# Layer 1's neighbourhood attention: query tiles of 8 rows by 16 columns, doubled buffers, and the normalisation on GpSimd

## What is computed

```
key_r = rs[:, None] + arange(8); key_c = cs[:, None] + arange(16)      # cs = clip(col - 8, 0, 48), rs = 0
q, k, v = split(h @ w_in); q = q * 64 ** -0.5                          # 16 heads, for latent and context tokens
s_n = einsum(q, k_latent[nbr_idx]) + rpb[:, rel_idx]                   # 128 neighbours of each query
s_c = einsum(q, k_context)                                             # 256 context keys
p = softmax(concat([s_n, s_c]))
out = (p[..., :128] @ v_latent[nbr_idx] + p[..., 128:] @ v_context) @ w_out
```

## Time and profile before

| | us |
|---|---|
| median of 3 runs | 3803.41 (3798.04 to 3803.81) |
| profiled execution, span of its instructions | 3800.5 |
| stage `na_in` in it | 1279.0 to 1461.5 |
| stage `attn_n` in it | 1461.5 to 1660.5 |
| stage `na_out` in it | 1660.5 to 1710 |
| TensorE busy, of the span | 3207.3 (84%) |
| VectorE, ScalarE, GpSimd busy | 1443.0, 784.6, 254.3 |
| transfers over the span | 675.97 MB, mean 178 GB/s |

### The profile page before, as it was taken

One profiled execution on the slowest core, in us unless ns is written; L12 is line 12 of the kernel. 1 busy time (PEld: TensorE's weight loads), 2 busy tenths in 40 slices (PEclk: granted clock), 3 DMA queues, 4 the chain that ended last, 5 costly groups with the idle time before them and its releaser, 6 DMA issues. The chain is left out here.

```text
span 3800.5 us, 48810 instructions
## 1 busy us (share of the span) xinstructions
PE 3207.3 (84%) x19239; PEld 2152.7 (57%) x19239; DVE 1443.0 (38%) x2444; ACT 784.6 (21%) x1496; POOL 254.3 (7%) x335
## 2 busy tenths in 40 slices
PE   7999988689886798785987657988999899689997
PEld 4534666333333696562333336856887687468876
DVE  2026673200000624653000006445564583455554
ACT  2013661111111303632111111142110111121101
POOL 0000110111111100001111110000000000000000
PEclk9998999899997799997998788998999899889998
DMA  7086813899997314008999984212342273023421
GB/s 278 1 299 164 206 35 117 308 393 392 400 403 308 129 56 100 1 23 312 391 404 407 409 331 141 67 40 78 92 120 68 48 105 56 23 78 99 121 62 50
DMA packets 315248, 675.97 MB, mean 178 GB/s; under 512 B 49939, under 2 KB 237429, under 8 KB 259640
## 3 DMA queue, kind: packets, MB, share of 16 engines
q1 hardware_dynamic: 299644, 636.32, 48.7%
q0 software_dynamic: 13344, 31.49, 2.5%
q10 hardware_dynamic: 2067, 5.48, 0.4%
HBM read 637.95 MB, written 47.05 MB: 180 GB/s over the span
## 5 line engine op out<-in xcount | busy, mean ns | idle before, releaser
L2054 DVE TENSOR_TENSOR moe0b_hidden<-moe0b_hidden,moe0b_wide_ps 64x512 f32<-64x512 f32 (+1 forms) x41 | 24.9, 607 | 492.1 <-ACT moe0b_hidden L2051 492.1
L2054 DVE TENSOR_TENSOR moe1b_hidden<-moe1b_hidden,moe1b_wide_ps 64x512 f32<-64x512 f32 (+1 forms) x36 | 20.6, 573 | 478.3 <-ACT moe1b_hidden L2051 478.3
L2039 PE MATMUL moe0b_wide_ps<-moe_raw,moe0b_feats 128*64 128x512 f32 x304 | 148.4, 640 | 33.7 <-DMA moe_raw<-in_moe_w_up 32.5
L2040 PE MATMUL moe0b_wide_ps<-moe_raw,moe0b_feats 128*64 128x512 f32 x304 | 148.8, 642 | 0.0
L2039 PE MATMUL moe1b_wide_ps<-moe_raw,moe1b_feats 128*64 128x512 f32 x208 | 104.9, 658 | 25.5 <-DMA moe_raw<-in_moe_w_up 24.4
L2039 PEld LDWEIGHTS moe0b_wide_ps<-moe_raw,moe0b_feats 128*64 128x64 f32 x304 | 42.3, 147 | 120.1 <-issue 118.0
L2040 PE MATMUL moe1b_wide_ps<-moe_raw,moe1b_feats 128*64 128x512 f32 x208 | 105.1, 660 | 0.0
L591 ACT ACTIVATE ln_squares<-all_x 128x512 f32<-128x512 f32 x32 | 19.3, 630 | 373.0 <-DVE all_x L641 373.0
L2024 PE MATMUL moe1b_wide_ps<-moe_raw,moe1b_feats 128*32 128x256 f32 x704 | 58.1, 491 | 44.5 <-DMA moe_raw<-in_moe_w_up 44.5
L1221 PE MATMUL attn_n_turned<-all_ident,attn_n_probs 128*128 128x128 f32 x384 | 57.2, 286 | 37.2 <-DVE attn_n_probs L1312 37.1
L2051 ACT ACTIVATE moe0b_hidden<-moe0b_wide_ps 64x512 f32<-64x512 f32 (+1 forms) x41 | 21.4, 522 | 319.2 <-PE moe0b_wide_ps L2040 248.7
(11 more groups left out here) (794 smaller groups left out, 8620.7 us busy)
## 6 DMA issues: line engine op xcount, KB each, us to landing
moe_raw<-in_moe_w_gate SPq DMA_DIRECT2D x88, 1024.0 KB, 28.4
moe_raw<-in_moe_w_up SPq DMA_DIRECT2D x88, 1024.0 KB, 29.1
moe_raw<-in_moe_w_down SPq DMA_DIRECT2D x88, 1024.0 KB, 28.5
all_ahead<-in_ffn_w_up SPq DMA_DIRECT2D x88, 512.0 KB, 5.0
all_h<-in_moe_w_gate SPq DMA_DIRECT2D x40, 1024.0 KB, 28.4
all_h<-in_w_ada SPq DMA_DIRECT2D x20, 1024.0 KB, 5.0
all_h<-in_moe_w_up SPq DMA_DIRECT2D x20, 1024.0 KB, 28.8
all_ahead<-in_moe_w_up SPq DMA_DIRECT2D x20, 1024.0 KB, 29.6
```

What stands on the lines that cost most here:

```text
L2039: nc.tensor.matmul(wide_ps[n][LOW, :], x[:, c, :], gate[:, at], start=c == 0, stop=c == DC - 1)
L2040: last = nc.tensor.matmul(wide_ps[n][HIGH, :], x[:, c, :], up[:, at], start=c == 0, stop=c == DC - 1)
L2054: return nc.vector.tensor_tensor(hidden[n][HIGH, 0:cols], hidden[n][HIGH, 0:cols], wide_ps[n][HIGH, 0:cols], ALU.mult)
```

## The change

A query tile is now 16 columns by all 8 rows. Since a query's window is at most 8 columns to either side, a tile sees 32 columns by 8 rows = 256 latent keys beside the 256 context keys, 512 instead of 768; there are 4 tiles to a pair of heads, 32 in all, as before.

- The latent tokens are put into column order by the norm `mod1` (`by_column`), so that q, k and v come out by columns. The attention's output is put back into row order when ScalarE takes it (`take_mixed`).
- Tiles 0 and 3 (edge tiles) see columns 0 to 31 and 32 to 63. Tiles 1 and 2 (inner tiles) see their own 16 columns and 8 on each side; `key_pieces` puts them in the places (own, right 8, left 8), and the scores of an inner tile take one product for each piece.
- For an inner tile's values the side columns of two 128-token tiles of v must be mixed; VectorE does it during `na_in` into free space of x (`WindowValues`), for which the v slabs now come first, then q, then k.
- The attention has a stage of its own, `neighbourhood_attention`: four score slots and four `raised`, `probs` is gone (GpSimd scales `raised` in place), TensorE scores two tiles ahead, and the division is GpSimd's (`tensor_scalar`, 64 of them).
- The bias store is [64 columns w, 2, 240, 16]. `WindowRows.pool` makes 32 columns in place of 64, in one operation or three, and the table has a row of 16 partitions for each grid row: 2 halves x 8 rows x 4 tiles = 64 transfers for heads 0 to 3, read at the end of `na_in` (`read_first`), and 64 for heads 4 to 15 at the start of the attention (`read_rest`), before the next weights. VectorE waits for all 64 of the first at tile 0, and for 16 of the rest at each of the tiles 8 to 11.

```diff
+def key_pieces(tile):
+    if tile in (0, COLUMN_TILES - 1):
+        return [(0, tile // 2 * KEY_COLS, KEY_COLS)]
+    own = tile * QUERY_COLS
+    return [(0, own, QUERY_COLS), (QUERY_COLS + HALF_COLS, own - HALF_COLS, HALF_COLS), (QUERY_COLS, own + QUERY_COLS, HALF_COLS)]
...
             for w in range(self.PER):
                 at = self.LAST - (w0 + w)
-                G.tensor_tensor(self.made[n][:, w, :], self.biases[:, n, at:at + GRID_W], self.outside[:, w0 + w, :], ALU.add).then_inc(self.ready, 1)
+                for place, col, cols in key_pieces(w0 // self.PER):
+                    last = G.tensor_tensor(self.made[n][:, w, place:place + cols], self.biases[:, n, at + col:at + col + cols],
+                                           self.outside[:, w0 + w, col:col + cols], ALU.add)
+                last.then_inc(self.ready, 1)
...
-            sp.dma_start(P.w_dram[w0:w0 + self.PER, n * R:(n + 1) * R, :].rearrange("w r c -> r w c"), self.made[n][:]).then_inc(self.stored[n], 16)
+            sp.dma_start(P.w_dram[w0:w0 + self.PER, :, n * R:(n + 1) * R, :].rearrange("w a r c -> r w a c"),
+                         self.made[n][:].rearrange("p w (a c) -> p w a c", a=2)).then_inc(self.stored[n], 16)
...
 class WindowTables:
+    FIRST = 4
+    def read(self, sp, table, heads, into):
+        rows = self.P.w_dram.rearrange("w a (h r) c -> w h a r c", r=REL_R)
+        for j in range(COLUMN_TILES):
+            for r in range(ROWS):
+                cols = slice(j * QUERY_COLS, (j + 1) * QUERY_COLS)
+                for a in range(2):
+                    sp.dma_start(table[r * QUERY_COLS:(r + 1) * QUERY_COLS, j, :, a * PART:(a + 1) * PART],
+                                 rows[cols, heads, a, WIN_R - 1 - r:REL_R - r, :].rearrange("w h r c -> w h (r c)")).then_inc(into(j), 16)
...
+    def wait(self, dve, i, j):
+        if i == 0 and j == 0:
+            dve.wait_ge(self.first_in, 32 * COLUMN_TILES * ROWS)
+        if 2 * i == self.FIRST:
+            dve.wait_ge(self.rest_in[j], 32 * ROWS)
...
+class WindowValues:
...
+        V.tensor_scalar(self.mixed[:, :, slab, :], self.v[:, CTX_T:CTX_T + 2, cols], self.sides[:, 0:1], None, ALU.mult).then_inc(self.left_ready, 1)
+        dve.wait_ge(self.left_ready, slab + 1)
+        V.scalar_tensor_tensor(self.mixed[:, :, slab, :], self.v[:, CTX_T + 2:TOK_T, cols], self.sides[:, 1:2], self.mixed[:, :, slab, :],
+                               ALU.mult, ALU.add).then_inc(self.ready, 1)
...
+def neighbourhood_attention(nc, P, tag, q, k, values, tables, ahead):
+    RING = 3
+        raised = [sb(f"raised{n}", [PART, KEYS])[:] for n in range(4)]
+        scores = [ps(f"scores{n}", [PART, KEYS]) for n in range(4)]
+        turned = [ps(f"turned{n}", [PART, CHUNKS, PART]) for n in range(RING)]
...
+        @block.sync
+            tables.read_rest(sp)
+            ahead.start(sp)
...
+        @block.tensor
+            def turn(n):
+                if n >= RING:
+                    pe.wait_ge(turned_taken, n - RING + 1)
+                pe.wait_ge(normed, n + 1)
...
+            score(0)
+            score(1)
+            for t in range(N):
+                if t + 2 < N:
+                    score(t + 2)
+                turn(2 * t)
+                if t:
+                    mix(t - 1)
+                turn(2 * t + 1)
+            mix(N - 1)
...
+        @block.vector
+            def find_top(n):
+                if s == 0:
+                    tables.wait(dve, i, j)
+                dve.wait_ge(scored, n + 1)
+                if n >= 4:
+                    dve.wait_ge(turned_ready, n - 3)
...
+        @block.gpsimd
+            for n in range(2 * N):
+                at = slot(n)
+                pool.wait_ge(shared, n + 1)
+                nc.gpsimd.tensor_scalar(raised[at], raised[at], share[:, at:at + 1], None, ALU.mult).then_inc(normed, 1)
...
+            split_stage(nc, P, "na_in", P.h, slabs, products, first, slab=slab, beside=side, later=tables.read_first)
```

More of the change, by code:

```diff
@@ L738, in modulate_jobs @@
         size=D,
+        by_column=by_column and t == LAT,
     ) for t, w in spans]
@@ L762, in __init__, with split_stage @@
         self.slab, self.operands, self.shape, self.take, self.engine, self.finish = slab, operands, shape, take, engine, finish
-def split_stage(nc, P, tag, x, slabs, products, first, engines=("act", "dve"), banks=8, beside=None, slab=None):
+def split_stage(nc, P, tag, x, slabs, products, first, engines=("act", "dve"), banks=8, beside=None, slab=None, later=None):
     n_x = x.shape[-1]
@@ L797, in _ @@
                     sp.dma_start(slot, source).then_inc(raw_in[h % 2], 16)
+            if later is not None:
+                later(sp)
         def result(n):
@@ L2371 @@
 class WindowTables:
[L2374 to L2382, removed]
@@ L2390, in neighbourhood_mixer @@
+def neighbourhood_mixer(nc, A, K, P, q, first, ahead, norms):
+    with ExitStack() as ctx:
+        sb, _, sem = scope(nc, ctx, "na")
         k = sb("k", [PART, DC, TOK])
         v = P.h[:].rearrange("p a b -> p (a b)").rearrange("p (t d) -> p t d", t=TOK_T)
[L2392 to L2403, removed]
@@ L2416, in neighbourhood_mixer @@
-        attention_stage(nc, P, "attn_n", turns, ahead, tables)
+        tables = WindowTables(P, sb, sem)
+        products, ends = [], []
+        PER = D // HALF_SLAB
+        mixed = P.x[:, :, 0:CTX].rearrange("p (g s) n -> p g s n", g=2)
+        slabs = window_slabs(P, A["na_w_in"][0])
+        for n in range(PER):
+            token_slab(nc, products, n, lambda t, n=n: v[:, t, n * HALF_SLAB:(n + 1) * HALF_SLAB], TOK_T)
+            ends.append(len(products) + 1)
+        for n in range(PER):
+            for j in range(2):
+                products.append(SplitProduct(
+                    PER + n, lambda w, x, j=j: [(w[:, c, j * PART:(j + 1) * PART], x[:, c, LAT]) for c in range(DC)], (PART, SEQ),
+                    copy_to(nc, q[:, 2 * n + j, :], HEAD ** -0.5)))
@@ new lines, in neighbourhood_mixer @@
+        for n in range(PER):
+            feature_slab(nc, products, 2 * PER + n, lambda j, at=n: k[:, 2 * at + j, :], wide(TOK))
+        with ExitStack() as low:
+            sb, _, sem = scope(nc, low, "na_v")
+            slab = FirstSlab(nc, P, first, sb, sem)
+            norm_stage(nc, P, "mod1", norms, 0, ahead=first, slab=slab)
+            side = WindowValues(nc, K, v, mixed, ends, sb, sem)
+            split_stage(nc, P, "na_in", P.h, slabs, products, first, slab=slab, beside=side, later=tables.read_first)
@@ L2419, in lat_norm_job, with window_slabs @@
+        neighbourhood_attention(nc, P, "attn_n", q, k, values, tables, ahead)
+def window_slabs(P, w):
+    return [[(raw_slab(P, n), rows_of(w)[:, :, at:at + HALF_SLAB])] for n, at in enumerate([*range(2 * D, 3 * D, HALF_SLAB), *range(0, 2 * D, HALF_SLAB)])]
 def lat_norm_job(P, gain, bias):
```

190 lines of the change are left out of this document (165 added, 25 removed).

## The result

The changed kernel takes 3750.2 us (median of 4 runs, 3748.2 to 3750.6), the kernel before 3803.6 beside it: a ratio of 0.9857, 95% interval 0.9842 to 0.9873, 53 us faster. Forecast were 3755 and 48 us. The profiled execution spans 3746.3 us (3800.5 before).

What follows compares the result with a forecast made beforehand. TensorE was taken to bound layer 1's attention at 3.5 us a tile. 3800.5 - 53 (attention) + 2 (in-projection) + 3 (layer 0) = 3752.5 us profiled, 3755 as median of runs; range 3722 to 3790.

Steps and rivals of the forecast that it cites:

- TensorE bounds at 3.5 a tile: Layer 1's attention: TensorE's scores, transposes and product with v sum to 3.5 us a tile and set the period.
- P: Layer 1's attention: time of one 128x512 GpSimd multiply, taken as 1.2 us between ends of 0.5 and 6.0.
- The loop's formula: Layer 1's attention: the loop through GpSimd takes 1.95 + P, 3.15 us, and decides the period from P = 1.55.
- The stage without late tables, 119: Layer 1's attention: 32 tiles of 3.5 give 112 us, filling and draining add some 7.
- The tables at 105 GB/s, two waits of 11 us, 4 for the clock, 27 in all: Layer 1's attention: later heads' tables arrive 15 us a part, TensorE idles 11 us twice, half clock adds 4; stage 146.
- In-projection +2: Layer 1's in-projection: with v first, TensorE starves waiting for the low parts of x; +2 us (0 to 4).
- Layer 0, +3: Layer 0's attention: GpSimd's longer burst of smaller bias-row operations slows VectorE and TensorE; +3 us (0 to 6).
- Its own signs: Attention: period 3.4-3.6, two 8-14 us idles, parts 15 us apart, multiply near 1.2; wrong if 10 apart or GpSimd always busy.
- Rival 1: Late tables: partitions do not matter, issue binds; only the fourth part 3 us late, stage 122, total 3731; chance 0.2.
- Rival 2: Late tables: transfers slower still, 57 to 85 GB/s; total 3802 at 57, 3777 at 75; chance 0.12.
- Rival 3: Attention: GpSimd binds at P of 2.2 to 2.9, or contends with VectorE; total 3762 to 3805; chance 0.13.
- Rival 4: Attention: GpSimd's multiply costs more than 2.9 us, up to 6.0; at 3.5 stage 236, total 3845; chance 0.05.

Runs made afterwards that it cites:

- e2: Changed kernel with the multiply by the reciprocal moved back from GpSimd to VectorE; layer 1's attention takes 134.8 us, against 140.3 in the changed kernel.
- e3: Changed kernel with six SBUF slots for raised scores instead of four, multiply still on GpSimd; layer 1's attention takes 137.6 us, period 3.35.
- e1: Changed kernel with the twelve later heads' tables not read, the first four heads' used instead; layer 1's attention takes 125.3 us, span 3721.5.
- e8: e2 with the twelve later heads' tables read in two groups, 128 transfers of 48 KB; 3720.6 us, ratio to the kernel before 0.9794.
- e6: Changed kernel with each of the 64 later transfers going to all 128 partitions in 512-byte runs, not the table's data; layer 1's attention takes 125.6 us.
- e7: Kernel before with each 64-column GpSimd bias sum made as three of 32, 16 and 16; layer 0's attention 220.0 us against 224.6, whole 3797.6.
- e9: Changed kernel with a tile's queries ordered by column, so each table transfer writes every eighth partition, not 16 neighbours; 3739.4 us, ratio to kernel before 0.9838.

## Why the prediction came out as it did

- **TensorE bounds at 3.5 a tile.** Wrong in the bound. TensorE needs 3.35 (e2, e3); pieces cost an inner tile 0.18 more than an edge tile, where 0.25 was taken. The period was 3.59, GpSimd's loop, because **P was 1.56 and not 1.2**. The step that failed is "a multiply by one scalar has one tensor input like the cast": the upper value between the two rates, 1.6, was the right one. The loop's formula was right to 0.08 us, and six slots in place of four take the loop away (e3).
- **The stage without late tables, 119.** It was 125.3 (e1): 3 from the period, the rest from filling and draining, where GpSimd's 1.56 us stands uncovered. Beside 32 periods the two ends take 10.4 us in e1 and 5.8 in e8, where VectorE multiplies; 7 was forecast.
- **The tables at 105 GB/s, two waits of 11 us, 4 for the clock, 27 in all.** The mechanism was right (e1, e6), the two waits came where they were foreseen (tiles 10 and 11); the size was 15.0 (e1). The rate was 115 to 142, and a slower period asks later. The rates that the prediction quotes from the Trainium skill, page "SBUF — State Buffer", section "Door 1: The DMA port swizzle", are both lower than what was measured here over many transfers: 104 GB/s for 16 neighbours against 115 to 142, and 196 for 64 partitions against the 227 that the prediction called agreement. The 4 us for the clock are not to be seen in e1, although the granted clock did fall to 0.66 and 0.63. So the stage was forecast 6 too short without the tables and their cost 12 too high: the 53 lies as near the measured 59 as it does because one error took back half of the other.
- **In-projection +2:** +2.1, of which the first chunks' waits for the low parts are only about 0.5; the rest was not tried.
- **Layer 0, +3:** wrong in sign, -4.6 (e7). The step that failed took the time lost in the earlier trace rows as proportional to the length of the burst. It hung on the length of each GpSimd instruction.
- **Its own signs.** Right were the period (3.59, TensorE busy for 28.5 of 30 us) and the two waits for tables, though 6.9 and 8.9 us and not 8 to 14. Wrong were GpSimd's multiply and layer 0. The last two parts of the table came 10.9 us apart, not 15, nearer to the 10 that the prediction named as a sign against itself; GpSimd was busy for 26.2 of 30 us, near the other such sign.
- **Rival 1** falls: the partitions do set the rate, though by where they lie (e6, e9). **Rival 2** falls by the rate. **Rival 3** was partly right: the period runs through GpSimd, but at P = 1.56 instead of 2.2, and by the loop and not because GpSimd is full (two multiplies are 3.12 of 3.59 us). Its contention did not come: VectorE's biased operation takes 484 ns beside a working GpSimd and 484 in e2 without it. The rule of the Trainium skill, page "SBUF — State Buffer", section "Who interferes with whom", that a VectorE instruction with at most one SBUF input, outside its two-port modes, does not contend with GpSimd agrees with these two numbers. **Rival 4** falls: 1.56, not over 2.9.
- **The sum:** attention 6 better, layer 0 7.6 better, and the profiled execution 7.4 worse in layer 2, which nothing in the change is shown to cause. 3752.5 was forecast for that execution and 3746.3 came; the median was 3750.2, inside the forecast's own range. That it lies only 5 us from 3755 is luck in part: errors of both signs cancel. Two of the rivals' totals do not follow from their stages by the prediction's own sum: rival 2 at 57 GB/s (stage 198) gives 3807 and not 3802, rival 3 3758 to 3803 and not 3762 to 3805. Neither matters here.

## What to carry to other kernels

When double buffers are added, look again at every other relief in the same change: here the four slots alone would have kept the multiply on VectorE and TensorE full, and the slower engine's 1.56 us in the loop cost 5.5 us beside late tables and 12.3 without them. Order transfers by when their data is asked for, not by how the destination is laid out (e8). If their rate is the limit, try destinations whose partitions are not neighbours, and look at what the issue then takes (e9). When one engine's burst slows another, try the same work in shorter instructions (e7).

## What the runs showed that was not expected

- GpSimd's multiply of 128x512 by a scalar per partition: 1549 to 1571 ns in 64 instances, 3.2 times VectorE's 486.
- VectorE's 128x768 SBUF-to-SBUF multiply took 1885 ns beside 64-column GpSimd sums of 339 ns and 625 beside sums of 16 and 32 columns of about 250. Waiting for one such sum would explain 0.34 us, not 1.26; why it takes so much longer is open.
- 16 neighbouring partitions: 121 GB/s and 8.3 us to land; 16 partitions eight apart: 148 GB/s, held by the issue, and 2.6 us, with issues of 0.60 us (median) in both of e9's groups.
- The same unchanged stage took 60.8 to 69.1 us in twelve profiled executions, with mean granted clocks of 0.89 to 0.73.
